# A two-model forward pass on one core: the order of norms, weight splits and sums where one matrix product hands over to the next

## What is computed

```python
def first_block(x, meta, ...):            # 16 meta tokens + 512 tokens, width 1024
    h = concat([meta, x])
    for i in range(2):
        hn = rmsnorm(h, g[0])
        m = rwkv_pool_mixer(hn, ...) if i == 0 else diff_attn_mixer(hn, ...)
        h = h + rmsnorm(m, g[1])
        f = square(relu(rmsnorm(h, g[2]) @ w1)) @ w2        # 1024 -> 4096 -> 1024
        h = h + rmsnorm(f, g[3])
    return h[:, 16:]

def second_block(x, mem, ...):            # 512 tokens
    u = rmsnorm(x, norm_mix_w) @ w_in
    x = x + concat([ssd_mixer(u_ssd), mla_mixer(u_mla)]) @ w_out
    x = x + memory_attention(rmsnorm(x), rmsnorm(mem), wq, wk, wv, wo)   # 4 heads, 256 memory rows
    x = x + conv_ffn(rmsnorm(x), w_up, conv_w, conv_b, w_down)  # 5632 wide, 3-tap causal convolution
    return rmsnorm(x, norm_final_w)       # silu(gate) * value between w_up and w_down
```

## Time and profile before

| | |
|---|---|
| median of three runs | 2468.69 us (2461.75 to 2469.94) |
| the profiled execution's own time | 2461.71 us |
| its span | 2459.9 us |
| PE busy | 2319.9 us, 94% |
| DVE / ACT / POOL busy | 1400.9 / 1068.8 / 509.0 us |
| DMA | 190.97 MB, mean 78 GB/s |

### The profile page before, as it was taken

How to read it: one execution, slowest core, us unless ns; L and a number is a source line. 1 busy time by engine, 2 the same in 40 slices (tenths; PEclk the granted TensorE clock), 3 DMA queues, 4 the chain that set the end, 5 groups by cost and what they waited for, 6 DMA issues and landing times. The chain is left out here.

```text
span 2459.9 us, 41910 instructions
## 1 busy us (share of the span) xinstructions
PE 2319.9 (94%) x16669; PEld 1669.1 (68%) x16669; DVE 1400.9 (57%) x2232; ACT 1068.8 (43%) x1857; POOL 509.0 (21%) x582
## 2 busy tenths in 40 slices
PE   7999879999999999899999899989989988899998
PEld 5889768888877776774445765656647876644445
DVE  5576567532367765476532476664646455687733
ACT  6435543222245656442223356367654463433322
POOL 0277540002224540520012301034330000000000
PEclk9999999999999998999999999999999999899999
DMA  4211122223112112023222212011022330222222
GB/s 166 88 36 36 36 69 103 104 104 103 61 63 70 45 52 69 31 78 123 98 103 88 101 69 88 33 61 44 1 69 103 130 112 18 86 103 103 82 98 78
DMA packets 38939, 190.97 MB, mean 78 GB/s; under 512 B 12176, under 2 KB 14608, under 8 KB 17624
## 3 DMA queue, kind: packets, MB, share of 16 engines
q1 hardware_dynamic: 37944, 186.08, 21.4%
q10 hardware_dynamic: 800, 2.20, 0.3%
HBM read 185.08 MB, written 3.19 MB: 77 GB/s over the span
## 5 line engine op out<-in xcount | busy, mean ns | idle before, releaser
L459 DVE SCALAR_TENSOR_TENSOR wsp<-raw_w,wsp 128x2048 f16<-128x2048 f32 (+2 forms) x188 | 404.5, 2152 | 197.4 <-ACT wsp L437 192.2
L418 PE MATMUL ps<-hn,wsp 128*128 128x512 f16 x1968 | 432.3, 381 | 6.9 <-DVEq L242 4.8
L437 ACT ACTIVATE wsp<-raw_w 128x2048 f16<-128x2048 f32 (+2 forms) x188 | 328.5, 1747 | 115.5 <-PE ps L416 48.2
L418 PEld LDWEIGHTS ps<-hn,wsp 128*128 128x128 f16 x1968 | 192.4, 98 | 236.1 <-DVEq L242 5.3
L413 PE MATMUL ps<-hn,wsp 128*128 128x256 f16 (+1 forms) x2592 | 307.3, 282 | 39.9 <-ACT big L476 21.2
L418 PE MATMUL ps<-big,wsp 128*128 128x512 f16 (+1 forms) x1740 | 342.2, 357 | 2.2 <-issue 1.6
L416 PE MATMUL ps<-hn,wsp 128*128 128x264 f16 x2880 | 334.6, 279 | 3.6 <-DVE hn L722 3.6
L416 PEld LDWEIGHTS ps<-hn,wsp 128*128 128x128 f16 x2880 | 282.7, 99 | 51.7 <-issue 4.7
L413 PEld LDWEIGHTS ps<-hn,wsp 128*128 128x128 f16 x2592 | 259.5, 101 | 84.6 <-issue 32.1
L418 PEld LDWEIGHTS ps<-big,wsp 128*128 128x128 f16 x1740 | 171.0, 99 | 162.9 <-issue 5.3
L413 PE MATMUL ps<-big,wsp 128*128 128x256 f16 (+1 forms) x2184 | 248.2, 275 | 1.4 <-ACT wk L2561 0.7
(11 more groups left out here) (428 smaller groups left out, 2966.7 us busy)
## 6 DMA issues: line engine op xcount, KB each, us to landing
raw_w<-slabs SPq DMA_DIRECT2D x162, 1024.0 KB, 5.0
raw_w<-slabs SPq DMA_DIRECT2D x10, 512.0 KB, 3.8
raw_w<-slabs SPq DMA_DIRECT2D x8, 384.0 KB, 5.0
h<-xin SPq DMA_DIRECT2D x2, 1056.0 KB, 7.1
out<-hn SPq DMA_DIRECT2D x8, 256.0 KB, 2.1
big<-memx ACTq DMA_DIRECT2D x1, 1024.0 KB, 4.8
sml<-small SPq DMA_DIRECT2D x1, 768.0 KB, 14.3
cst<-consts SPq DMA_DIRECT2D x1, 582.0 KB, 13.1
```

Of the source, the lines that this page charges most:

```text
L418: mm = L.eng.matmul(two(ps[:rows, b, 0:T]), lhsT, rhs, start=first, stop=last)
L437: L.fin(L.eng.activation(wsp[:, n % NW, 0, lo:hi], raw_w[:, q % 2, at:at + hi - lo], ACT.Copy, scale=WSCALE), "hi")
L459: ins = L.eng.scalar_tensor_tensor(wsp[:, n % NW, 1, lo:hi], raw_w[:, q % 2, at:at + hi - lo], WSCALE, wsp[:, n % NW, 0, lo:hi], ALU.mult, ...
```

## The change

Five edits:

1. `gemm_grid` gets `sums_at` and `spread_at`: PE issues the sums and the spreading of half 1 behind steps 32 and 44 (was 12 and 24) in the three "post" heads (both mlps, `second_pe`) and behind steps 16 and 24 (was 8 and 13) in the ffn's head. The other "late" head (memory query) keeps 8 and 13.
2. In `grid_tail_*`: DVE does crossings 0 and 1, then the passes 0 to 7 in a row, with crossings 2 and 3 behind pass 3 and both half slabs behind pass 4; crossings 4 and 5 follow the passes, 6 and 7 stand in `mlp_dve`. ACT does both half slabs at m = 3 with pass 4 between them. POOL does the square adds of tiles 4 to 7 between its low parts and the crossing adds of tiles 4 to 7 last (`post_add(..., which)`).
3. In the heads (`mlp_*`, `second_*`, ffn): the whole of the next slab is split first, in one go; the roots of half 1 come on ACT behind output tile 2, the passes of half 1 behind output tiles 5, 6 and 7. In the ffn's head the roots follow the split.
4. Memory attention: the split of a head's two tiles stands in the loop, behind units 70, 71, 74, 75, 78 and 79; the last two tiles follow the loop.
5. Ffn: the tiles 0 to 3 are convolved by token halves, the first halves ahead of the loop; slab 2 is split whole behind m = 3. In the "late" tail of `w_mem_o` both high halves come at m = 3, the low halves at m = 3 and m = 5.

The hunk of `second_act`'s head, which is that of `mlp_act` with `x_unit` for `relu_half`, is left out.

```diff
@@ -505,7 +505,7 @@
         def gemm_grid(L, cnt, kt, nm, rhs, T, src=None, halved=False, head=None, tail=None, after=None, between=None,
-                      first_k=0):
+                      first_k=0, sums_at=8, spread_at=13):
@@ -540,7 +540,10 @@
-                            norm_step_pe(L, cnt, T, 1, head, done[z], 24)
+                            if done[z] == sums_at:
+                                norm_sums_pe(L, cnt, T, 1, head)
+                            if done[z] == spread_at:
+                                norm_spread_pe(L, cnt, T, 1, head)
@@ -551,11 +554,11 @@
-        def norm_step_pe(L, cnt, T, z, kind, done, spread=18):
+        def norm_step_pe(L, cnt, T, z, kind, done):
             if done == (12 if kind == "post" else 8):
                 norm_sums_pe(L, cnt, T, z, kind)
-            if done == (spread if kind == "post" else 13):
+            if done == (18 if kind == "post" else 13):
@@ -784,7 +787,7 @@
-        def post_add(L, cnt, T, m, z):
+        def post_add(L, cnt, T, m, z, which=(0, 1)):
@@ -793,13 +796,15 @@
-            for acc in (rs, acc2):
-                q = cnt["post_sq"] = cnt.get("post_sq", -1) + 1
-                L.take("post_sq")
-                add(acc, sq[:, q % 2, cols], "sq_added")
-            u = cnt["cross"] = cnt.get("cross", -1) + 1
-            L.take("cross")
-            add(acc3, cross[:, u % 2, cols], "cross_added")
+            if 0 in which:
+                for acc in (rs, acc2):
+                    q = cnt["post_sq"] = cnt.get("post_sq", -1) + 1
+                    L.take("post_sq")
+                    add(acc, sq[:, q % 2, cols], "sq_added")
+            if 1 in which:
+                u = cnt["cross"] = cnt.get("cross", -1) + 1
+                L.take("cross")
+                add(acc3, cross[:, u % 2, cols], "cross_added")
@@ -1122,7 +1127,7 @@
         def mlp_pe(L, cnt, src, T):
-            gemm_grid(L, cnt, 8, 32, src, T, src="hn", halved=True, head="post")
+            gemm_grid(L, cnt, 8, 32, src, T, src="hn", halved=True, head="post", sums_at=32, spread_at=44)
@@ -1150,7 +1155,8 @@
-            gemm_grid(L, cnt, 8, 16, n2, SEQ, src="hn", halved=True, head="post", after=after_tile)
+            gemm_grid(L, cnt, 8, 16, n2, SEQ, src="hn", halved=True, head="post", after=after_tile, sums_at=32,
+                      spread_at=44)
@@ -1419,7 +1425,7 @@
-            gemm_grid(L, cnt, 8, 44, n2, SEQ, src="hn", halved=True, head="late")
+            gemm_grid(L, cnt, 8, 44, n2, SEQ, src="hn", halved=True, head="late", sums_at=16, spread_at=24)
@@ -1917,9 +1923,11 @@
                 if m == 0:
                     post_roots_act(L, T, 0)
                     post_root2_act(L, T, 0)
-                for j in ((), (0,), (1, 2), (3,), (4,), (5,), (6, 7), ())[m]:
+                for j in ((), (0,), (1, 2), (3,), (), (5,), (6,), (7,))[m]:
                     pass_act(L, T, 0, j, dst, y)
-                if m in (3, 4):
+                if m == 3:
+                    split_hi_part(L, cnt)
+                    pass_act(L, T, 0, 4, dst, y)
                     split_hi_part(L, cnt)
         def trig_act(L):
@@ -1940,14 +1948,13 @@
-            split_hi_part(L, cnt)
-            post_roots_act(L, T, 1)
-            post_root2_act(L, T, 1)
-            split_hi_part(L, cnt)
-            relu_half(0, 0)
-            for m in range(1, 8):
+            split_hi(L, cnt)
+            for m in range(8):
                 relu_half(m, 0)
-                for j in ((), (0,), (1, 2), (3, 4), (5, 6), (7,), ())[m - 1]:
+                if m == 2:
+                    post_roots_act(L, T, 1)
+                    post_root2_act(L, T, 1)
+                for j in {5: (0,), 6: (1, 2), 7: (3, 4, 5, 6, 7)}.get(m, ()):
@@ -2245,9 +2251,11 @@
                 late_unit_act(L, cnt, m, 1)
                 if m == 0:
                     late_root_act(L, SEQ)
-                for j in ((), (0, 1), (2, 3), (4,), (5, 6), (7,), (), ())[m]:
+                for j in ((), (0, 1), (2, 3), (4,), (), (6,), (7,), ())[m]:
                     pass_act(L, SEQ, 0, j, n2)
-                if m in (3, 4):
+                if m == 3:
+                    split_hi_part(L, cnt)
+                    pass_act(L, SEQ, 0, 5, n2)
                     split_hi_part(L, cnt)
             raw = wk[:, WK0:WK0 + 8 * SEQ].rearrange("p (a b) -> p a b", a=8)
@@ -2261,13 +2269,14 @@
-            split_hi_part(L, cnt)
+                if z == 0 and m < 4:
+                    L.tell("raw")
+            split_hi(L, cnt)
             late_root_act(L, SEQ)
-            split_hi_part(L, cnt)
             raw_half(0, 0)
             for m in range(1, 8):
                 raw_half(m, 0)
-                for j in ((0,), (1, 2, 3), (4, 5, 6), (7,), (), (), ())[m - 1]:
+                for j in ((), (), (0, 1), (2, 3), (4, 5), (6,), (7,))[m - 1]:
@@ -2620,15 +2629,20 @@
                     first_half(m)
                 else:
                     post_cross(L, dcnt, T, y, gain, hx, m, 0)
-            for m in range(8):
-                post_cross(L, dcnt, T, y, gain, hx, m, 1)
-                if m == 0:
-                    post_tiny_dve(L, T, 0)
-                    root_inverse_dve(L, T)
-                for j in ((), (0,), (1, 2), (3,), (4,), (5,), (6, 7, 8), ())[m]:
-                    pass_dve(L, T, 0, j, hx, dst, gain2, y, gain, last_lo=4)
-                if m in (3, 4):
+            post_cross(L, dcnt, T, y, gain, hx, 0, 1)
+            post_tiny_dve(L, T, 0)
+            root_inverse_dve(L, T)
+            post_cross(L, dcnt, T, y, gain, hx, 1, 1)
+            for j in range(DT):
+                pass_dve(L, T, 0, j, hx, dst, gain2, y, gain, last_lo=4)
+                if j == 3:
+                    post_cross(L, dcnt, T, y, gain, hx, 2, 1)
+                    post_cross(L, dcnt, T, y, gain, hx, 3, 1)
+                if j == 4:
                     split_lo_part(L, dcnt)
+                    split_lo_part(L, dcnt)
+            post_cross(L, dcnt, T, y, gain, hx, 4, 1)
+            post_cross(L, dcnt, T, y, gain, hx, 5, 1)
         def head_tiny_dve(L, T):
@@ -2661,8 +2675,10 @@
         def mlp_dve(L, hx, nx, T, y, g, g2):
             gain = lambda at: lambda j: V("norm_g", at + j)
             split_lo_part(L, dcnt)
+            post_cross(L, dcnt, T, y, gain(g - 8), hx, 6, 1)
+            post_cross(L, dcnt, T, y, gain(g - 8), hx, 7, 1)
+            split_lo_part(L, dcnt)
             head_tiny_dve(L, T)
-            split_lo_part(L, dcnt)
             for j in range(DT):
                 pass_dve(L, T, 1, j, hx, nx, gain(g), y, gain(g - 8), last_lo=0)
             for m in range(32):
@@ -2692,22 +2708,22 @@
-        def conv_dve(L, dst, src, name, tile, ntile, taps, bias):
+        def conv_dve(L, dst, src, name, tile, ntile, taps, bias, lo=0, hi=SEQ):
             w = lambda j: V(name, j * ntile + tile)
-            last = L.eng.tensor_scalar(dst, src, w(taps - 1), V(bias, tile), ALU.mult, ALU.add)
+            last = L.eng.tensor_scalar(dst[:, lo:hi], src[:, lo:hi], w(taps - 1), V(bias, tile), ALU.mult, ALU.add)
             for d in range(1, taps):
                 L.step(last)
-                last = L.eng.scalar_tensor_tensor(dst[:, d:SEQ], src[:, 0:SEQ - d], w(taps - 1 - d), dst[:, d:SEQ],
-                                                  ALU.mult, ALU.add)
+                at = max(lo, d)
+                last = L.eng.scalar_tensor_tensor(dst[:, at:hi], src[:, at - d:hi - d], w(taps - 1 - d),
+                                                  dst[:, at:hi], ALU.mult, ALU.add)
...
         def second_dve(L, acc_next):
...
-            split_lo_part(L, dcnt)
+            split_lo(L, dcnt)
             head_tiny_dve(L, SEQ)
-            split_lo_part(L, dcnt)
@@ -2903,6 +2919,11 @@
+            def memory_split(j):
+                dve.wait_ge(sem("out_read"), 68 + 4 * (j // 2))
+                L.step(dve.tensor_copy(sc[:, j % 2, 0:SEQ], n2(j)))
+                split_dve(L, sc[:, j % 2, 0:SEQ], n2(j), "memo")
@@ -2913,10 +2934,10 @@
-            dve.wait_ge(sem("out_read"), 80)
-            for j in range(8):
-                L.step(dve.tensor_copy(sc[:, j % 2, 0:SEQ], n2(j)))
-                split_dve(L, sc[:, j % 2, 0:SEQ], n2(j), "memo")
+                if n >= 70 and n % 4 >= 2:
+                    memory_split(2 * (n // 4) - 34 + n % 4 - 2)
+            memory_split(6)
+            memory_split(7)
@@ -2924,21 +2945,28 @@
-                for j in ((), (0, 1), (2, 3), (4,), (5, 6), (7, 8), (), ())[m]:
+                for j in ((), (0, 1), (2, 3), (4, 5), (), (6,), (7, 8), ())[m]:
                     pass_dve(L, SEQ, 0, j, h2, n2, gain)
-                if m in (3, 4):
+                if m in (3, 5):
                     split_lo_part(L, dcnt)
+            split_lo(L, dcnt)
             root_inverse_dve(L, SEQ)
-            split_lo(L, dcnt)
...
+            def ffn_tile(m):
+                return 2 * (m // 4) + m % 2 + (FT2 if m % 4 >= 2 else 0)
+            for m in range(4):
```

(28 more changed lines are left out.)

13 lines of the change are left out of this document (6 added, 7 removed).

## The result

The changed kernel takes 2433.06 us, the median of 4 runs (2429.43 to 2439.13), beside 2469.32 for four runs of the kernel before: a ratio of 0.986, interval 0.983 to 0.989. The forecast was 2432. The profiled execution of the changed kernel is its slowest run, 2439.13 (span 2437.3), so it is compared by stretches and not by its end.

What follows compares the result with a forecast made beforehand. A chain, no full engine, bounds the kernel. Gains of 6.3 + 8.5 + 8.9 + 2.3 + 3.9 + 6.3 = 36.2 us off the median 2468.69 give 2432.5, forecast 2432; range of 8 in 10 2413 to 2450.

Steps and rivals of the forecast that it cites:

- What bounds the kernel: Whole kernel: no engine is full, a chain binds; a wait costs twice where the clock falls behind it.
- First mixer to first mlp: First mixer's tail into first mlp's head: PE starts 5.7 us earlier, clock costs 2.7; gain 6.3 us.
- Second mixer to second mlp: Same code at the second mixer's end, with 512 tokens: new start 1039.8, clock costs 2.7; gain 8.5 us.
- Second mlp to the second block: Second block's head: the 5.26 us wait at step 12 and the low clock behind it go; gain 8.9 us.
- Memory attention: Memory output product starts behind the last unit, 6.3 us less; splits in the loop cost 4.0; gain 2.3 us.
- Memory output to the ffn: Ffn's start: DVE ends the slab at 2088.8, PE starts at 2088.9, clock costs 2.5; gain 3.9 us.
- first convolutions: Ffn's slab 2: first token halves run earlier, at 1.25 us per half convolution; gain 6.3 us.
- The page's rule: DVE's new row of passes: two-SBUF-input operations and POOL's adds block each other, costing 9.6 us, giving 2442; one chance in eight within a rival.
- The crossings come too late: Rival, sums at step 32: crossings 3 us late at three places, clock falls again; gain 22, 2446; chance 0.22.
- Too short for the clock to fall: Rival: remaining waits leave the clock up and memory splits fit in the lead; gain 48.1, 2420; chance 0.15.
- Only moved: Rival: ffn and memory give nothing, heads lose their gain in the half-1 group; gain under 7, 2465; chance 0.05.
- Slower: Rival, half-1 group: low parts take 2.74 us each in a chain, 42 us in all; 2474; chance 0.03.

Runs made afterwards that it cites:

- x_busy: The kernel before, with matmuls whose result nobody reads added in PE's waits at both mlps' starts and the second block's sums: 2483.03 us, ratio 1.006.
- r_head: The changed kernel with the heads behind both mixers and the second mlp as before (sums at step 12, spreading at 24, split in halves, earlier passes): 2453.78 us.
- r_mem: The changed kernel with the splits of the memory attention's eight tiles behind the loop again: 2431.77 us, ratio 0.985.
- r_conv: The changed kernel with whole convolutions for the ffn's first four tiles and slab 2's halves behind m = 2 and 3 again: 2439.14 us.
- x_alt: The changed kernel with the first six memory splits one each behind units 71, 73, 75, 77, 78 and 79: 2433.94 us, ratio 0.987.
- x_lock: The changed kernel with five phases behind its last store, POOL adding beside an idle DVE or four kinds of DVE operation: 2465.38 us in one execution.
- r_tail: The changed kernel with only the order in the two mixers' output tails undone (crossings among passes, half slabs behind tiles 3 and 4): 2442.49 us.

## Why the prediction was right, step by step

- **What bounds the kernel.** Right: no engine got less work, and shorter waits gave the gain, with the clock behind them at the second block's head (2.85 and 1.3 us) and at the ffn's slab 2 (2.7, from 309.2 to 306.5 us between the first 512-column product and the end). That a wait costs twice was an inference from one pair of rows; x_busy showed that the slow matmuls are the clock's. The cost is not a fixed one: behind the mixers the shorter waits had 1.0 to 2.6 us of it, where 9.87 us of wait had 1.8.
- **First mixer to first mlp**, 6.3 forecast, 6.5 measured. The start came 5.5 us sooner behind the tail's sums (28.3 for 33.8) where 5.7 was said. Wrong in detail: the sums were ready 1.2 us later than said (42.1 us behind the tail's, 40.9 forecast), and the clock, counted at 2.7 us, cost 1.2 in one profile (12.47 us for 96 matmuls, 11.2 at the full clock) and 2.6 in the other (13.84). The forecast had the sums at 42.1 us, set by PE's 32 steps; 42.1 came out in both, once set by POOL's adds and once by PE's steps. That the number fits so closely is luck.
- **Second mixer to second mlp**, 8.5 forecast, 6.9 and 8.6 measured. The start came 6.3 sooner for 5.6; the sums at 38.6 us behind the tail's, for 39.2 said. The clock cost 1.0 us here in both profiles (11.92 and 11.95 us for 96 matmuls, 10.9 at the full clock) and not 2.7, so PE waited 1.70 and 1.65 for POOL, where no wait was forecast. In the first profile the clock fell again behind that wait, 1.7 us on 36 matmuls, and that is the difference between 6.9 and 8.6.
- **Second mlp to the second block**, 8.9 forecast, 8.7 measured: 5.26 of wait went, 2.85 and 1.3 of clock (the sums 1.40 for 2.72), and 0.41 for the place of output tile 3 came, 0.7 forecast; these add up to 9.0, 0.3 more than measured. The 8.7 rest on one profile of the kernel before; r_head, with the old head, had 75.5 for its 77.0, by which the gain is 7.2.
- **Memory attention**, 2.3 forecast, 0.9 measured with like clock ahead of the edit (1.0 against r_mem). The earlier start of the output product brought what was said (from the last unit to the tail's sums 24.3 us for 30.7, so 6.4; 6.3 forecast). The term that was mis-sized is the price of the splits in the loop: up to the last unit 134.3 us for 128.8, so 5.5; 4.0 forecast. PE stood still for 3.5 us more, about as counted, but was busy for 2.1 us more, which I had at nothing: behind the wait of 2.33 the clock fell. Where it did not, in r_conv, the price was 4.7. x_alt, without that wait, wins 2.1 us more.
- **Memory output to the ffn**, 3.9, and **first convolutions**, 6.3: together 10.2 forecast, 9.9 measured. r_conv divides them: 5.2 for the convolutions, so 4.7 for the start, a difference and not a run of its own. The start's two parts were off the same way: the clock cost 1.6 us (7.08 for 48 matmuls, 5.5 at the full clock), 2.5 forecast, and PE's spreading waited 0.33 for the root inverse, which set it. I had a half convolution at 1.25 us; it takes 1.46, and the next operation starts 1.61 behind its start (DVE of the changed kernel):

```profile
2115.90 0.41 DVE L2714 TENSOR_SCALAR wk<-wk,par 128x256 f32<-128x256 f32 x1
2116.35 1.01 DVE L2718 SCALAR_TENSOR_TENSOR wk<-wk,par 128x256 f32<-128x256 f32 x2
```

  From start to start, a first half takes 1.49 and a second 1.61, 3.10 together, 0.8 us more than the 2.28 of a whole. The four second halves ahead of slab 2 so took 1.4 us more than counted, and it came 1.80 late; I had said not over 1 us.
- **The page's rule** would have given 2442. Its mechanism is here: at the second mixer's end DVE and POOL show

```profile
1030.55 5.44 DVE L459 SCALAR_TENSOR_TENSOR wsp<-raw_w,wsp 128x2048 f16<-128x2048 f32 x2
...
1036.66 0.94 DVE L870 TENSOR_TENSOR h<-h,wk 128x256 f32<-128x256 f32 x1
```

```profile
1028.19 5.65 POOL L798 TENSOR_TENSOR wk<-wk 128x256 f32<-128x256 f32 x4 [3.00 <-DVE wk L787]
1033.92 2.60 POOL L901 TENSOR_TENSOR hn<-wk,hn 128x256 f16<-128x256 f32 x1
...
1049.72 3.69 POOL L798 TENSOR_TENSOR wk<-wk 128x256 f32<-128x256 f32 x2 [0.43 <-DVE wk L787]
```

  (the splits 5.44 us for 4.62, a residual add 0.94 for 0.42, a low part 2.60, two adds of 3.69 beside a split). Its price was off: what the three passes behind the splits lose lies beside PE's wait and amounts to under 1 us (their residual adds took 0.94, 0.60 and 0.55 for 0.42), since POOL slips in between two half slabs, as the alternation in x_lock has it, where I had it stand behind both.
- **Rivals.** *The crossings come too late*: in part, waits of 1.37 and 1.70 us at L748 where hardly one was forecast; behind the 1.70 the clock fell in one of two profiles. *Too short for the clock to fall*: false, it fell behind the 4.1 us of both mlps in every profile, if for less time than counted, and behind 2.33 in most. *Only moved*: true of the tail's edit alone (r_head), half true of the heads' alone (r_tail: 2.1 and 2.7 us gained in A and B), false of the two together. *Slower*: the half-1 group showed no wait over 0.75 us.

## What to carry to other kernels

Where a wait sits between two products, look for the schedule that spans all engines: an earlier start was worth nothing (2 us lost in A) while the heads were the old ones, and sums put back to step 12, with the roots left in their new late place, cost the whole gain, 36.6 us. Measure such edits by a stretch between two marks of the bounding engine; some repeated within 0.3 us (C, E), others within 1.7 to 4.1 (A, D, B), where totals move by 10 and more; and list the falls of the clock in each, since two executions differ by them. And of work that must stand in a lead, put one piece at each gap: two in a row made a wait of 2.33 us, behind which the clock fell in seven of eight profiles; one at a time made 1.03 at most, and it fell in none of three.

## What was not expected of the hardware

How long the granted clock stays down behind the same wait, and whether it falls, differs between executions of the same code. Behind 4.14 us it was at half for 3.1 us of work in one and 5.9 in the next; behind 2.33 it fell in seven of eight (4 matmuls in 1.87 us for 1.03); behind 1.70 it fell, behind 1.65 not. It was below 1 in stretches in which PE never stood still: 0.81 over 205 to 245 us, with 40.00 us of PE busy. Two engines that exclude each other do so one operation at a time, so each long operation of VectorE holds up one add of GpSimd's (5.9 us for three splits), and a short one of VectorE doubles (828 ns for 424). What sets the clock in the unchanged part stays open; no run here was made for it.
